# Stick-breaking and differential attention in one launch: masks of the two score components in another order, and another order of work around the first pair, the last pair and the last head

## The chip, the cores and the metric

One core of a Trainium2 chip runs the whole program, a decoder trunk of two layers on 512 tokens of width 1024, in float32. The metric is device time in microseconds, from one launch. TensorE (PE in the profile) does every product, VectorE (DVE), ScalarE (ACT) and GpSimd (POOL) prepare its operands and take its results, SyncE (SP) loads the weights.

## The reference

```python
def stick_breaking_layer(x, norm_g, w_in, w_out):
    q, k, v, gate = split(rms_norm(x, norm_g) @ w_in, 4)      # 16 heads of 64
    z = q @ k.T / 8                                           # strictly causal
    a = exp(log_sigmoid(z) + suffix_sum(log_sigmoid(-z)))
    return (silu(gate) * (a @ v)) @ w_out

def diff_layer(x, k, v, norm_g, w_in, q_norm_g, lam_params, subln_g, w_out, ...):
    q, gate = split(rms_norm(x, norm_g) @ w_in, 2)            # 8 heads, two components of 64
    q = apply_rope(rms_norm(q, q_norm_g), cos, sin)
    a = softmax(q1 @ k1.T / 8) - lam * softmax(q2 @ k2.T / 8) # causal
    o = rms_norm(a @ v, subln_g) * (1 - lam_init)
    return (silu(gate) * o) @ w_out

x = x + stick_breaking_layer(x, ...)
k, v = shared_kv(x, ...)
x = x + diff_layer(x, k, v, ...)
```

## The kernel before

Every product of float32 numbers is made of three: each operand is split into a rounded part (`..._hi`) and the rest (`..._lo`), and TensorE adds hi·hi, hi·lo and lo·hi (`three`, L637 to L639). So each slab of weights, 128 rows by 512 columns, is loaded by SyncE into `w_raw`, rounded into `w_hi` by POOL (`split`, L514) or by ACT (`slab_hi`, L1126, for the slabs in the list `ACT_HI`), and POOL subtracts it for `w_lo` (L516, or L504 behind ACT). The slabs are numbered in the order of their use; a ring of six buffers serves the first layer and a ring of four the second. All order is written by hand: each engine has its own list of work, and semaphores tie the lists together.

**The first layer** runs over eight pairs of heads. In `pair(p)` TensorE makes the scores into six banks, then the projection of this pair's gate and of the next pair's q and k. Between them stand the suffix sums of each of the two heads (`suffix_sums`, L777 and L780), which wait until DVE has written the three `lo` pieces of that head (L1711, semaphore `s_sl`), and then the products with the values (`attend_a`, L794). Before the second of these TensorE waits for `s_qk`, the split of the next pair's k (`k_lo_a`, L1640). POOL splits the values of a pair (`values_a`, L528 and L532) and six slabs for the pair after. From the second pair on, those six slabs start only after the third `lo` piece of the pair; for the first pair they start right behind the values. The last pair is written apart (`last_pair`): it has the first slabs of the output matrix between its steps.

**The second layer** runs over eight heads. Head 0 and 1 and the last two are written apart, 2 to 5 run in a loop. `head(h)` on TensorE: `scores_b(h)` puts six masks (L735, L737) into six banks and adds the scores of both components onto them (L970). Component c has the banks 2b+c for b = 0, 1, 2. Then come the projection of a gate, the values of the head before (`attend_b`), and half a projection of the q two heads on, then the turning of that projection's squares into bank 1 and of the squares of the last output into bank 3 (`turned_squares`), the turning of the probabilities into the banks of the first component (`turn_probs`), and the other half. `o_roots` spreads the roots of an output's mean squares into bank 7.

DVE in `head(h)`: for each b a maximum over the two banks (L1944) and a small product that gives ACT the bias of its exponentials (L1949, `s_nb`); `o_scale` (L1924), which scales the output two heads back and is waited for by `attend_b`; the gate; the combination of the two components' probabilities (L1960 to L1965); `o_times_gate` (L1931); the `lo` parts of the probabilities (L1996); and `turned_means`, which sums the squares in bank 1 (L1907) and bank 3 (L1909), adds the small terms (L1910, L1912: `s_rq`), and after ACT's root (`head_root`, L1131 and L1133) refines it (`newton`, L1576 to L1578: `s_rb`). `gate_log` (L1650) and `gate_silu` (L1656) are the two steps of a gate on DVE, `gate_exp` (L1242) the one of ACT between them. The gate of head 6 is the 15th; its buffers are `g32_7` and `ge_7`.

In the last head TensorE has no projection left. It makes tile after tile of the product with the output matrix (`early_tile`), two slabs, `o_roots`, two more slabs, then `attend_b`.

## Time and profile before

| | us |
|---|---|
| median of 3 runs | 626.11 (625.68 to 628.41) |
| profiled execution | 624.4 |
| its span, first to last instruction | 623.2 |
| PE busy | 604.3 (97%) |
| PE weight loads busy | 508.9 (82%) |
| DVE busy | 455.7 (73%) |
| ACT busy | 375.2 (60%) |
| POOL busy | 330.0 (53%) |
| granted TensorE clock, mean | 0.997 |

A matmul of 512 columns is listed with about 0.39 us, but they are pipelined: back to back one starts 0.23 us after another. So the time that TensorE loses at a wait is the distance of two starts less the usual step, a little more than the idle time in brackets.

### The profile page before, as it was taken

The numbers are of one execution on the slowest core, as the hardware profiler recorded it, in microseconds if no ns is written. First come the engines' busy times: TensorE is split into PE (matmuls) and PEld (weight loads), VectorE is DVE, ScalarE is ACT, GpSimd is POOL, SyncE is SP. The second block draws the span as 40 slices with busy tenths as digits, with TensorE's granted clock in tenths as the row PEclk, the third lists the DMA queues.
The fourth block names the chain that finished last, engine by engine and source line by source line (L and its number), as shares of the span: only waits on it lengthen the run. The fifth ranks groups of instructions, "written<-read, shape, count | busy, mean of one in ns | idle before, by whom it ended". The sixth has DMA issues, their size and how long they took to land.

```text
span 623.2 us, 9903 instructions
## 1 busy us (share of the span) xinstructions
PE 604.3 (97%) x3204; PEld 508.9 (82%) x3204; DVE 455.7 (73%) x734; ACT 375.2 (60%) x814; POOL 330.0 (53%) x313
## 2 busy tenths in 40 slices
PE   6999999999999999999999999999999999997998
PEld 6888887888888888878888888888878878886886
DVE  2389498988989898884337799435889888888441
ACT  5662695786968668684446644325667776685420
POOL 4639366757556475625353555557454465434261
PEclk9999999999999999999999999999999999998999
DMA  7424312213122121212212332230421222121142
GB/s 257 127 85 121 101 34 68 69 37 98 34 67 67 34 84 44 74 35 68 68 64 72 96 106 86 84 109 24 125 83 45 75 84 78 57 69 34 35 150 87
DMA packets 61439, 48.83 MB, mean 78 GB/s; under 512 B 7521, under 2 KB 48609, under 8 KB 61409
## 3 DMA queue, kind: packets, MB, share of 16 engines
q1 hardware_dynamic: 60368, 48.44, 25.4%
q8 instruction: 17, 0.28, 0.2%
q10 hardware_dynamic: 1040, 0.00, 0.1%
q14 instruction: 14, 0.11, 0.1%
HBM read 44.24 MB, written 2.10 MB: 74 GB/s over the span
## 4 chain that ended last, share of the span: by engine, by line
PE 81%; DVE 13%; issue 2%; ACT 2%; DMA 1%; POOL 0%; DVEq 0%; SPq 0%; ACTq 0%
PE bank L637 21%; PE bank L639 21%; PE bank L638 21%; PE bank L780 4%; PE bank L794 3%; PE bank L756 3%; DVE small L1944 2%; PE bank L970 1%; DVE lo L1733 1%; DVE lo L1711 1%; PE bank L777 1%; DMA xs<-in_x 1%; PE bank L990 1%; DVE sp L1697 1%; PE bank L675 1%
## 5 line engine op out<-in xcount | busy, mean ns | idle before, releaser
L504 POOL TENSOR_TENSOR w_lo<-w_raw,w_hi 128x512 fp32r<-128x512 f32 x80 | 108.5, 1368 | 154.0 <-ACT w_hi L1126 115.2
L637 PE MATMUL bank<-h_hi,w_hi 128*128 128x512 f32 x320 | 129.3, 404 | 0.7 <-ACT q L1379 0.7
L637 PE MATMUL bank<-w_hi,h_hi 128*128 128x512 f32 x320 | 127.5, 398 | 1.6 <-POOL w_lo L504 1.5
L639 PE MATMUL bank<-h_hi,w_lo 128*128 128x512 f32 x320 | 125.5, 392 | 0.0
L639 PE MATMUL bank<-w_hi,h_lo 128*128 128x512 f32 x320 | 125.1, 391 | 0.0
L638 PE MATMUL bank<-h_lo,w_hi 128*128 128x512 f32 x320 | 125.1, 391 | 0.0
L638 PE MATMUL bank<-w_lo,h_hi 128*128 128x512 f32 x320 | 124.8, 390 | 0.0
L516 POOL TENSOR_TENSOR w_lo<-w_raw,w_hi 128x512 fp32r<-128x512 f32 x80 | 112.3, 1404 | 6.4
L514 POOL CAST w_hi<-w_raw 128x512 fp32r<-128x512 f32 x80 | 59.0, 738 | 75.8 <-DVE lo L1711 35.7
L1126 ACT ACTIVATE w_hi<-w_raw 128x512 fp32r<-128x512 f32 x80 | 48.9, 630 | 55.7 <-PE bank L639 55.5
L637 PEld LDWEIGHTS bank<-h_hi,w_hi 128*128 128x128 f32 x320 | 60.1, 188 | 14.4 <-ACT q L1379 1.1
L637 PEld LDWEIGHTS bank<-w_hi,h_hi 128*128 128x128 f32 x320 | 60.1, 188 | 14.4 <-issue 2.1
L639 PEld LDWEIGHTS bank<-h_hi,w_lo 128*128 128x128 f32 x320 | 60.0, 188 | 13.6
L639 PEld LDWEIGHTS bank<-w_hi,h_lo 128*128 128x128 f32 x320 | 60.1, 188 | 13.1
L638 PEld LDWEIGHTS bank<-w_lo,h_hi 128*128 128x128 f32 x320 | 60.2, 188 | 11.8
L638 PEld LDWEIGHTS bank<-h_lo,w_hi 128*128 128x128 f32 x320 | 60.2, 188 | 11.6
L1733 DVE TENSOR_TENSOR lo<-ex,hi 128x512 fp32r<-128x512 f32 (+1 forms) x48 | 48.6, 1065 | 3.6 <-ACT hi L1280 3.6
L1506 ACT ACTIVATE pr<-bank,small 128x512 f32<-128x512 f32 (+3 forms) x64 | 38.7, 617 | 15.8 <-DVE small L1949 15.8
L1711 DVE TENSOR_TENSOR lo<-sp,hi 128x512 fp32r<-128x512 f32 (+1 forms) x48 | 41.1, 882 | 0.0
L1697 DVE SCALAR_TENSOR_TENSOR sp<-bank,ex 128x512 f32<-128x512 f32 (+1 forms) x48 | 27.3, 597 | 5.9 <-ACT ex L1263 5.6
L1831 DVE TENSOR_TENSOR xs<-bank,xs 128x512 f32<-128x512 f32 x16 | 10.9, 692 | 28.1 <-PE bank L639 28.1
L1944 DVE TENSOR_REDUCE small<-bank 128x2 f32<-128x1024 f32 (+3 forms) x32 | 25.5, 818 | 7.2 <-PE bank L970 7.2
(217 smaller groups left out, 1191.4 us busy)
## 6 DMA issues: line engine op xcount, KB each, us to landing
w_raw<-in_a_w_in SPq DMA_DIRECT2D x64, 256.0 KB, 2.8
w_raw<-in_w_kv SPq DMA_DIRECT2D x32, 256.0 KB, 3.0
w_raw<-in_b_w_in SPq DMA_DIRECT2D x32, 256.0 KB, 2.7
w_raw<-in_a_w_out SPq DMA_DIRECT2D x16, 256.0 KB, 2.6
w_raw<-in_b_w_out SPq DMA_DIRECT2D x16, 256.0 KB, 2.8
xs<-in_x SPq DMA_DIRECT2D x4, 512.0 KB, 6.1
qrot<-qs SPq DMA_DIRECT2D x32, 64.0 KB, 2.0
out_x<-xs SPq DMA_DIRECT2D x8, 256.0 KB, 2.7
```

Of the source, the lines that this page charges most:

```text
L504: nc.gpsimd.tensor_tensor(w_lo[s][:, :], w_raw[s][:, :], w_hi[s][:, :].bitcast(F32), ALU.subtract).then_inc(s_w, 1)
L514: nc.gpsimd.tensor_copy(w_hi[s][:, :], w_raw[s][:, :]).then_inc(s_whi, 1)
L516: nc.gpsimd.tensor_tensor(w_lo[s][:, :], w_raw[s][:, :], w_hi[s][:, :].bitcast(F32), ALU.subtract).then_inc(s_w, 1)
L637: pe.matmul(o, ahi, bhi, start=start, stop=False, skip_group_check=True)
L638: pe.matmul(o, ahi, blo, start=False, stop=False, skip_group_check=True)
L639: return pe.matmul(o, alo, bhi, start=False, stop=stop, skip_group_check=True)
L1126: A(w_hi[s][:, :], w_raw[s][:, :], ACT.Copy).then_inc(s_whia, 1)
L1506: A(pr[c][:, cols(at, w)], bank[BANK_B[c, b]][:, cols(at - BANKS[b][0], w)], ACT.Exp, bias=tiny[:, 8 + 2 * i + c:9 + 2 * i + c], scale=mea ...
L1697: STT(out=sp[m // 3][:, seg], in0=bank[m][:, 0:BANKS[m % 3][1]], scalar=0.0, op0=ALU.max, in1=ex[m // 3][:, seg], op1=ALU.add).then_inc(s_ ...
L1711: TTN(lo[h][:, seg], sp[h][:, seg], hi[h][:, seg].bitcast(F32), ALU.subtract).then_inc(s_sl, 1)
L1733: TTN(lo[h][:, seg], ex[h][:, seg], hi[h][:, seg].bitcast(F32), ALU.subtract).then_inc(s_al, 1)
L1944: ins = V.tensor_reduce(tiny[:, 2 * i:2 * i + 2], banks[:, 2 * b:2 * b + 2, cols(at - BANKS[b][0], w)], AX.X, ALU.max)
```

## The change

Three things are changed.

1. In `scores_b` the masks are laid in the order first component b = 0, 1, 2, then the second component's b = 2, 0, 1. The one wait for `s_rq` is gone. Bank 1 waits for a new semaphore, `s_mq` (the squares of q are summed), bank 3 for another, `s_mo` (those of the output are). `turned_means` raises them at the two sums, which now follow each other without a wait between; DVE waits for both behind them.
2. For the last head: ACT makes the root before the two slabs instead of after. DVE takes `gate_log` of the 15th gate ahead of the root's refinement, `gate_silu` of it to behind the last bias, and `o_scale` of head 5 to before the third maximum. POOL makes its two slabs before `value_lo`, and drops a wait for `s_rb`.
3. POOL, first pair: the last four of six slabs wait for `s_qk` at 4, the split of the second pair's k. POOL, last pair: the slabs from `G_OUT + 4` on wait for `s_sl` at 44, the second `lo` piece of that pair.

```diff
@@ gpsimd
-        for g in range(G_BODY + 6, G_BODY + 12):
+        split(G_BODY + 6)
+        split(G_BODY + 7)
+        pool.wait_ge(s_qk, 4)
+        for g in range(G_BODY + 8, G_BODY + 12):
             split(g)
...
         values_a(KT - 1)
+        pool.wait_ge(s_sl, (KT - 1) * 6 + 2)
         for g in range(G_OUT + 4, N_A):
             split(g)
...
-        pool.wait_ge(s_rb, KT)
-        value_lo(KT - 2)
         split(H_OUT + 2)
         split(H_OUT + 3)
+        value_lo(KT - 2)
         value(KT - 1)
@@ tensor, scores_b
-            if not first:
-                pe.wait_ge(s_rq, h + (R_HEAD - 1))
-            for c in (1, 0):
-                for b in range(3):
-                    if c == 0 and not first:
+            for c, b in ((0, 0), (0, 1), (0, 2), (1, 2), (1, 0), (1, 1)):
+                if not first:
+                    if c == 0:
                         pe.wait_ge(s_al, h * 3 + (46 + b))
-                    mask(bank[BANK_B[c, b]][:, :], (3 * P, 2 * P, P)[b], len(BANK_STRIPS[b]), P, mask_b)
+                    elif b == 0:
+                        pe.wait_ge(s_mq, h)
+                    elif b == 1 and not second:
+                        pe.wait_ge(s_mo, h - 1)
+                mask(bank[BANK_B[c, b]][:, :], (3 * P, 2 * P, P)[b], len(BANK_STRIPS[b]), P, mask_b)
@@ scalar, last head
                 gate_copies(h, later, 2 * KT - 2)
+                head_root(h - 1, False, False)
                 slab_hi(H_OUT + 2)
                 slab_hi(H_OUT + 3)
-                head_root(h - 1, False, False)
@@ vector
-            st.link(V.tensor_reduce(means[:, 0:8], comps(bank[1][:, :]), AX.X, ALU.add))
+            V.tensor_reduce(means[:, 0:8], comps(bank[1][:, :]), AX.X, ALU.add).then_inc(s_mq, 1)
             if with_o:
-                st.link(V.tensor_reduce(means[:, 8:12], bank[3].rearrange("p (t d) -> p t d", d=P), AX.X, ALU.add))
+                V.tensor_reduce(means[:, 8:12], bank[3].rearrange("p (t d) -> p t d", d=P), AX.X,
+                                ALU.add).then_inc(s_mo, 1)
+            dve.wait_ge(s_mq, h + 1)
+            if with_o:
+                dve.wait_ge(s_mo, h)
...
             for b in range(3):
+                if b == 2 and not q_next:
+                    o_scale(h - 2)
...
-            if n_before == 2:
+            if not q_next:
+                gate_silu(2 * KT - 1, g32_7, ge_7)
+            elif n_before == 2:
                 o_scale(h - 2)
...
+            if silu_first:
+                gate_log(2 * KT - 1, g32_7, ge_7)
             root_newton(c0, c1, h + R_HEAD).then_inc(s_rb, 1)
...
         head(KT - 2, 2, q_after=False, silu_first=True)
-        gate_log(2 * KT - 1, g32_7, ge_7)
-        gate_silu(2 * KT - 1, g32_7, ge_7)
```

On PE, the masks of the last head's scores (those of heads 2 to 6 alike; the line numbers of the changed file are 5 higher here), before:

```order
L735 MATMUL bank<-mask_b,ident_r 128x128 [waits norm_sum_ready,v_split,qk_split]
L737 MATMUL bank<-mask_b,ident_r 128x256
L735 MATMUL bank<-mask_b,ident_r 128x128
L735 MATMUL bank<-mask_b,ident_r 128x128 [waits weights_split]
L737 MATMUL bank<-mask_b,ident_r 128x256 [waits weights_split]
L735 MATMUL bank<-mask_b,ident_r 128x128 [waits weights_split]
```

and after:

```order
L740 MATMUL bank<-mask_b,ident_r 128x128 [waits weights_split,v_split,qk_split]
L742 MATMUL bank<-mask_b,ident_r 128x256 [waits weights_split]
L740 MATMUL bank<-mask_b,ident_r 128x128 [waits weights_split]
L740 MATMUL bank<-mask_b,ident_r 128x128
L740 MATMUL bank<-mask_b,ident_r 128x128 [waits q_squares_added]
L742 MATMUL bank<-mask_b,ident_r 128x256 [waits output_squares_added]
```

The wait that stood before all six masks, `norm_sum_ready`, is gone, and the two that replace it stand before the last two.

On DVE, between the sums of head 6 (L1910, L1912) and the first combination of the last head, before:

```order
L1576 TENSOR_TENSOR small<-small 128x12 [waits norm_root_ready]
L1577 SCALAR_TENSOR_TENSOR small<-small 128x12 [waits dve_steps]
L1578 SCALAR_TENSOR_TENSOR small<-small 128x12 [waits dve_steps]
L2006 SCALAR_TENSOR_TENSOR small<-small 128x4
L1650 SCALAR_TENSOR_TENSOR ge<-g_7,ge 128x512 [waits gate_log1p,dve_steps]
L1656 TENSOR_TENSOR silu<-g_7,ge 128x512 [waits gate_sigmoid]
L1944 TENSOR_REDUCE small<-bank 128x2 [waits scores_ready]
...
L1949 SCALAR_TENSOR_TENSOR small<-small 128x2x2 [waits dve_steps]
L1944 TENSOR_REDUCE small<-bank 128x2 [waits scores_ready]
L1949 SCALAR_TENSOR_TENSOR small<-small 128x2 [waits dve_steps]
L1924 TENSOR_TENSOR og<-ot,bank 128x512 [waits output_roots_spread]
```

and after:

```order
L1657 SCALAR_TENSOR_TENSOR ge<-g_7,ge 128x512 [waits gate_log1p]
L1583 TENSOR_TENSOR small<-small 128x12 [waits norm_root_ready]
L1584 SCALAR_TENSOR_TENSOR small<-small 128x12 [waits dve_steps]
L1585 SCALAR_TENSOR_TENSOR small<-small 128x12 [waits dve_steps]
L2023 SCALAR_TENSOR_TENSOR small<-small 128x4
L1957 TENSOR_REDUCE small<-bank 128x2 [waits scores_ready,dve_steps]
...
L1962 SCALAR_TENSOR_TENSOR small<-small 128x2x2 [waits dve_steps]
L1935 TENSOR_TENSOR og<-ot,bank 128x512 [waits output_roots_spread]
L1957 TENSOR_REDUCE small<-bank 128x2 [waits scores_ready]
L1962 SCALAR_TENSOR_TENSOR small<-small 128x2 [waits dve_steps]
L1663 TENSOR_TENSOR silu<-g_7,ge 128x512 [waits gate_sigmoid]
```

Both steps of the 15th gate have left the place between the root and the first maximum, and `og` stands one maximum and one bias earlier.

On POOL, the third and fourth of the six slabs in the first pair, before:

```order
L514 CAST w_hi<-w_raw 128x512 [waits slab_loaded5,slab_used]
L516 TENSOR_TENSOR w_lo<-w_raw,w_hi 128x512 [waits slab_hi_split]
L514 CAST w_hi<-w_raw 128x512 [waits slab_loaded0,slab_used]
L516 TENSOR_TENSOR w_lo<-w_raw,w_hi 128x512 [waits slab_hi_split]
L514 CAST w_hi<-w_raw 128x512 [waits slab_loaded1,slab_used]
```

and after:

```order
L516 CAST w_hi<-w_raw 128x512 [waits slab_loaded5,slab_used]
L518 TENSOR_TENSOR w_lo<-w_raw,w_hi 128x512 [waits slab_hi_split]
L516 CAST w_hi<-w_raw 128x512 [waits slab_used,qk_split,slab_loaded0]
L518 TENSOR_TENSOR w_lo<-w_raw,w_hi 128x512 [waits slab_hi_split]
L516 CAST w_hi<-w_raw 128x512 [waits slab_loaded1,slab_used]
```

The third slab, and with it everything that POOL has after it, waits for `qk_split`.

## Rows read from the trace of the kernel before

**Rows 1.** The page, busy time by engine and costliest groups (busy, mean ns).

```profile
PE 604.3 (97%) x3204; PEld 508.9 (82%) x3204; DVE 455.7 (73%) x734; ACT 375.2 (60%) x814; POOL 330.0 (53%) x313
...
L516 POOL TENSOR_TENSOR w_lo<-w_raw,w_hi 128x512 fp32r<-128x512 f32 x80 | 112.3, 1404 | 6.4
L514 POOL CAST w_hi<-w_raw 128x512 fp32r<-128x512 f32 x80 | 59.0, 738 | 75.8 <-DVE lo L1711 35.7
```

**Rows 2.** Waits of PE: waiting line, releaser, us in total, times, longest.

```profile
PE bank L735 <- DVE small L1912: 3.7, 6, 0.7
PE bank L637 <- DVE og L1924: 2.0, 1, 2.0
PE bank L794 <- DVE k_lo L1640: 1.5, 1, 1.5
PE bank L637 <- POOL w_lo L504: 1.5, 2, 0.8
...
PE bank L780 <- DVE lo L1711: 0.6, 1, 0.6
```

**Rows 3.** Timeline of PE, heads 3 and 4: start, duration, line, idle before.

```profile
481.83 0.39 PE L639 MATMUL bank<-h_hi,w_lo 128*128 128x512 f32 x1
482.75 0.33 PE L735 MATMUL bank<-mask_b,ident_r 128*128 128x128 f32 x1 [0.54 <-DVE small L1912]
...
483.58 0.50 PE L970 MATMUL bank<-k_hi,q_hi 64*128 64x512 f32 x2
...
500.90 0.39 PE L639 MATMUL bank<-h_hi,w_lo 128*128 128x512 f32 x1
```

**Rows 4.** Timeline of DVE, head 3.

```profile
484.95 1.23 DVE L1944 TENSOR_REDUCE small<-bank 128x2 f32<-128x1024 f32 x1 [0.57 <-PE bank L970]
...
490.96 1.06 DVE L1961 SCALAR_TENSOR_TENSOR small<-small 128x2 f32<-128x2 f32 x1
...
500.88 0.69 DVE L1909 TENSOR_REDUCE small<-bank 128x4 f32<-128x512 f32 x1
```

**Rows 5.** Timeline of POOL, head 3.

```profile
484.49 1.29 POOL L580 TENSOR_TENSOR vb_lo<-v,vb_hi 128x512 fp32r<-128x512 f32 x1 [2.24 <-DVE small L1578]
...
490.37 1.63 POOL L540 TENSOR_TENSOR k_lo<-k,k_hi 128x512 fp32r<-128x512 f32 x1 [0.19 <-POOL k_hi L538]
```

**Rows 6.** Timeline of PE, last head.

```profile
569.69 0.79 PE L637 MATMUL bank<-at_hi,vb_hi 128*128 128x512 f32 x1 [1.95 <-DVE og L1924]
...
573.10 0.44 PE L637 MATMUL bank<-w_hi,h_hi 128*128 128x512 f32 x1
...
575.89 0.95 PE L899 MATMUL bank<-small,osq 128*128 128x1 f32 x8
```

**Rows 7.** Windows: length, PE, weight loads, DVE, ACT, POOL, granted clock, DMA.

```profile
569.70:573.10 3.40, 3.40 (x13) 3.11 (x13) 2.81 (x8) 2.09 (x10) 0.00 (x0) 0.53 0.00 0
```

**Rows 8.** Timeline of DVE, last head.

```profile
565.43 1.21 DVE L1944 TENSOR_REDUCE small<-bank 128x2 f32<-128x1024 f32 x1
...
568.96 0.68 DVE L1924 TENSOR_TENSOR og<-ot,bank 128x512 f32<-128x512 f32 x1
```

**Rows 9.** Timeline of ACT, last head.

```profile
559.80 1.15 ACT L1126 ACTIVATE w_hi<-w_raw 128x512 fp32r<-128x512 f32 x2
560.84 0.21 ACT L1131 ACTIVATE small<-small 128x12 f32<-128x12 f32 x1
```

**Rows 10.** Timeline of PE, second pair of the first layer.

```profile
111.32 0.40 PE L780 MATMUL bank<-hi,neg_tri 128*128 128x512 f32 x1
```

**Rows 11.** Timeline of DVE: first and second pair; last, a later stretch without POOL.

```profile
95.05 3.61 DVE L1733 TENSOR_TENSOR lo<-ex,hi 128x512 fp32r<-128x512 f32 x3
98.58 0.68 DVE L1640 TENSOR_TENSOR k_lo<-bank,k_hi 128x512 fp32r<-128x512 f32 x1
...
109.13 0.42 DVE L1711 TENSOR_TENSOR lo<-sp,hi 128x256 fp32r<-128x256 f32 x1
...
279.01 1.63 DVE L1733 TENSOR_TENSOR lo<-ex,hi 128x512 fp32r<-128x512 f32 x3 [1.04 <-ACT hi L1280]
```

More of the change, by code:

```diff
@@ L331, in build @@
     s_or = sem("output_roots_spread")
+    s_mq = sem("q_squares_added")
+    s_mo = sem("output_squares_added")
     s_rb = sem("norm_roots_ready")
@@ L949, in _, with scores_b @@
                     turn_keys(turn_after[grp * KT + k])
-        def scores_b(h, first):
+        def scores_b(h, first, second=False):
             pe.wait_ge(s_qk, h + (2 * KT + 1))
             pe.wait_ge(s_v, KT + 1 if first else h * 2 + KT)
-            if not first:
-                pe.wait_ge(s_rq, h + (R_HEAD - 1))
-            for c in (1, 0):
-                for b in range(3):
-                    if c == 0 and not first:
-                        pe.wait_ge(s_al, h * 3 + (46 + b))
-                    mask(bank[BANK_B[c, b]][:, :], (3 * P, 2 * P, P)[b], len(BANK_STRIPS[b]), P, mask_b)
+            for c, b in ((0, 0), (0, 1), (0, 2), (1, 2), (1, 0), (1, 1)):
+                if not first:
+                    if c == 0:
+                        pe.wait_ge(s_al, h * 3 + (46 + b))
+                    elif b == 0:
[3 more added lines that the diff above has]
+                mask(bank[BANK_B[c, b]][:, :], (3 * P, 2 * P, P)[b], len(BANK_STRIPS[b]), P, mask_b)
             for b in range(3):
@@ L1019, in head @@
             if n_before:
-                scores_b(h, False)
+                scores_b(h, False, n_before == 1)
             def roots():
@@ L2017, in _ @@
         with dve.Fori(2, KT - 2) as i:
-            st.enter(i, 2, 12)
+            st.enter(i, 2, 10)
             head(i, 2)
```

4 lines of the change are left out of this document (2 added, 2 removed).

## The prediction, made before the changed kernel was timed

> **What bounds the kernel now.** I read the page first: TensorE is busy for 604.3 of 623.2 us [rows 1], so no other engine bounds the whole, and only time in which TensorE stands still can be won. Then its waits [rows 2]. Besides the first load of x, five releasers are in reach of the change: the sums of squares (3.7 us in 6 waits, one for each of heads 2 to 7), the scaled output `og` in the last head (2.0), the k split of the first pair (1.5), POOL's slabs in the last head (1.5), a `lo` piece in the last pair (0.6). Then the timelines around each, since a wait is worth what the next thing that comes late leaves of it.
>
> By the distance of starts a wait costs a little more than its listed idle time: in head 3 the last projection matmul starts at 481.83, the next could start 0.23 later, at 482.06, and the first mask starts at 482.75: 0.69 lost [rows 3].
>
> **Masks, heads 2 to 7.** In steady heads TensorE's own work from the first score matmul to the end of the projections runs from 483.58 to 500.90 + 0.23 = 501.13, 17.55 us [rows 3]. The six masks take 483.58 − 482.75 = 0.83. If nothing made it wait, a head would be 18.38; it is 19.15 now. Of the new order, the masks of three banks wait for probabilities split before the sums, so they are free at once; so is the fourth. The last waits for the second sum, which ends at 500.88 + 0.69 = 501.57 [rows 4]. Seen from that head's projection end, 501.13, five masks last to about 501.8, so in the first such head the wait goes entirely, 0.8 us.
>
> Then something else is late. DVE does not simply move up with the scores. POOL starts its chain when the root is refined (484.49), and that hangs on the end of TensorE's projection through ACT, not on the scores. DVE's small product L1961 starts at 490.96 and takes 1.06, ending at 492.02, just after POOL's `k_lo` ends at 490.37 + 1.63 = 492.00 [rows 4, 5]: it stood behind POOL. So DVE's path to the second sum is fixed to the projection end P: L1961 ends at P + 9.96, the second sum 9.55 later; the removed wait between the two sums gives 0.12 back. The sum ends at P + 19.4. The last mask starts then, the scores 0.2 later at P + 19.6. With g the time from a projection's end to the scores, the period is 17.55 + g and the scores of the next head stand at P + 17.55 + 2g, so 2g = 2.05, g about 1.03, period 18.58 instead of 19.15. That is 0.57 a head in the middle. Head by head: 0.8, 0.25 (DVE has not moved yet), 0.57 three times, and about 0.8 for the last, where DVE has slack. Sum: **3.5 us**. Bounds: 6 × 0.77 = 4.6 if TensorE bounds every head; 1.8 if only the two small terms behind the sums are saved (0.3 a head).
>
> **Last head.** Before: first maximum at 565.43, `og` from 568.96 to 569.64, values product from 569.69, 3.41 us long, to 573.10; then a tile to 575.89 and the sums of head 6's output [rows 6, 8]. After, with the projection end 2.7 earlier (3.5 less the last head's own 0.8), at 555.8: ACT copies the gate until 557.06 and makes the root at once. The two slabs cost 1.04 there before, 560.84 − 559.80 [rows 9]; they now stand behind it. DVE refines until 558.2 and finds the scores done. Gone from between are both gate steps. The first maximum starts at 558.3, 7.1 us earlier. It ends at 559.5. POOL's slab and `value_lo` chain now begins at about 558.1 and ends at about 561.9, since nothing holds it, and the bias product meets the second slab: I charge 1.1 us, as L1961 above. Second maximum and bias: 562.0. `og` one maximum earlier: 562.7. TensorE has its scores, two tile steps, the spread roots and two more steps done at 562.1 (the two slab waits, 1.5 us [rows 2], go, because the slabs no longer stand behind `value_lo` and DVE's root), so 0.7 us of waiting is left of 2.0. It starts at 562.8 instead of 569.69.
>
> The values product then: it took 3.41 us at a granted clock of 0.53, the level of 1.2 GHz, after three waits within 6 us [rows 6, 7]. With one short wait ahead I take the level of 2.4 GHz and 1.85 us. So it ends at 564.65 and the next tile at 567.45. Now DVE is late: third maximum, bias, 15th `gate_silu` (moved here, 0.6), and the combination, beside POOL's split of the last values, which may start at 564.7 and stalls two of its products for about 1.9 in all; `ot` is ready at 569.2. TensorE waits 1.75 where it did not wait. It makes the sums at 569.2 instead of 575.89: **6.7 us** earlier, of which 3.5 came from the masks and 3.2 are the last head's own. From there everything is tied to TensorE as before; the later slab of the ring stays 0.25 late as it is. Bounds: 9.1 in all if POOL stalls nothing; 4.2 if the masks give 2.5 and half the clock's 1.56 and an additional 0.7 of waiting stay.
>
> **POOL, last pair.** POOL's two slabs stood in DVE's way to the third `lo` piece; the wait is 0.6 listed [rows 2], 0.75 by starts. Held until the second piece, they meet only short operations. TensorE needs them 3 us later, after the suffix sums, with about 1 us to spare. **−0.7**, bounds −0.75 and 0.
>
> **POOL, first pair.** Here one wait goes and another comes. The k split starts at 98.58 because two groups of three `lo` pieces took 3.61 (and the one before as long) beside POOL, where three take 1.63 alone [rows 11]. With only two slabs made, the k split ends at 97.2, before TensorE comes at 97.7: −1.64 by starts (1.5 listed [rows 2]). But four slabs and the values are now made from 97.3 on. At the page's means, 1.40 + 0.74 a slab [rows 1], and 2.2 for the values, POOL is busy until about 108. That is where DVE has its stretch up to the third `lo` piece of the second pair, which ended at 109.13 + 0.42 = 109.55, with 1.77 to spare before TensorE's 111.32 [rows 10, 11]. TensorE comes at 109.68 now. DVE could be done at about 107.1; six or seven of its operations meet one of POOL's, and a meeting costs (3.61 − 1.63)/3 = 0.66, 4.3 in all: 111.4. So TensorE waits about 1.75, and all that was won is gone. DVE then runs late by 1.9 until its next k split, 16 us on: a further wait of about 0.9. Net **+1.0**. Bounds: −1.6 (DVE slips through) and +1.9.
>
> For that row the Trainium skill has a sharper price. "SBUF — State Buffer", in its section on the ports, says that a VectorE instruction with two SBUF inputs and a GpSimd one that reads SBUF exclude each other for a whole instruction, by the order of issue. Were every meeting a full slab operation, the mean of 1.40 and 0.74, the 4.3 would be 7.0 by that rule, and the first pair would come out at +3.7 instead of +1.0. The trace shows 0.66, since most meetings begin halfway, so I stay with the row.
>
> **Sum.** +1.0 − 0.7 − 6.7 = −6.4. The profiled execution took 624.4 (span 623.2): 618.0. The median of the runs is 1.7 above it, so 626.1 − 6.4 = **619.7 us**.
>
> **The rivals.**
>
> *More: POOL stalls little.* In the last head DVE's small products slip between POOL's operations, and the first pair keeps half of its 1.64. For it: half of the bias products in heads 2 and 3 are short. Against: L1961 is stalled in every head. 9.1 + 0.7 + 0.2 = 10.0: 616.1.
>
> *Less: the last head waits again.* TensorE waits for `ot` 1.75 or more after a wait for `og`, and the clock is granted at half again, as in [rows 7]. That keeps 1.56 and a second wait of 0.7: 622.0.
>
> *The masks change nothing but their place.* The second sum ends only 0.3 before the semaphore that is dropped; were the first five masks not laid meanwhile (they wait for the probabilities' split), six heads would give 1.8 instead of 3.5, and the lag would cost the last head another 1.5. 623.0. Against: those splits end 1.4 before.
>
> *Slower: DVE never catches up after the first pair.* POOL's held slabs push DVE's third `lo` piece behind TensorE's need, and if each pair has as much work for DVE as time, the lag of 1.75 returns in each of pairs 1 to 6: 6 × 1.75 − 1.64 = +8.9 against the −7.4 of the rest, 627.6. It decides from the fifth repetition. Against it: DVE idles some 2 us in each later pair, and TensorE waits for it in none of them.
>
> **How the numbers follow.** Forecast 0.50 (618 to 621.5); more 0.17; less 0.17; masks only moved 0.08; slower 0.05; something else 0.03. 615.5 reaches to the first rival, 623.0 takes in the second and third; about 0.15 is left out. What a measurement of this kernel can tell from no change is about 0.5%, 3.1 us, so 623.0. Faster by more: 0.50 + 0.17 + 0.14 + 0.03 = 0.84. Slower by more than 629.2: 0.04. Same: 0.12.
>
> **What the changed profile would show.** Right: in heads 3 to 6 the last mask, not the first, has a wait, of 0.2 to 0.4, on the second sum, and the period of the scores is near 18.6; the first maximum of the last head begins about 7 us earlier, and its values product runs at 0.23 us a matmul; a wait for `ot` of 1 to 2 us stands before the sums of head 6's output; L794 no longer waits in the first pair, but L780 waits in the second. Wrong: if heads are 18.4 long, POOL does not fix DVE's path; if they are 19.1, it is the masks' rival; if L780 doesn't wait, DVE and POOL get along better than I charge, and 1 to 2.6 us more are won; if L780 waits in several pairs, the slower rival is at work.

## The result, and the profile after

| | before | changed |
|---|---|---|
| median of 4 runs each, same chip | 627.0 us (625.68 to 628.41) | 617.25 us (617.12 to 619.89) |
| ratio, 95% interval | | 0.9869 (0.9844 to 0.9894) |
| profiled execution | 624.4 | 617.12 |
| its span | 623.2 | 615.9 |

The changed kernel is 1.3% faster, and the interval of the ratio does not reach 1. 619.7 was forecast, 617.25 came: inside the range of 615.5 to 623, but 0.75 below the band of the forecast itself (618 to 621.5). Of the profiled execution 618.0 was forecast and 617.12 came. The page of the changed kernel, with the lines that answer to [rows 1]:

```profile
PE 602.7 (98%) x3204; PEld 507.9 (82%) x3204; DVE 453.1 (74%) x734; ACT 375.5 (61%) x814; POOL 328.0 (53%) x313
...
L518 POOL TENSOR_TENSOR w_lo<-w_raw,w_hi 128x512 fp32r<-128x512 f32 x80 | 111.1, 1389 | 6.4
L516 POOL CAST w_hi<-w_raw 128x512 fp32r<-128x512 f32 x80 | 58.6, 732 | 80.4 <-DVE lo L1718 31.5
```

The same work is done in the same busy time; what went is idle time of TensorE. Its waits besides the first load of x (line, releaser: us in all, times, longest), to be read against [rows 2]:

```profile
PE bank L904 <- DVE ot L1942: 1.1, 1, 1.1
PE bank L924 <- DVE pr L1980: 1.0, 1, 1.0
PE bank L785 <- DVE lo L1718: 0.9, 1, 0.9
PE bank L642 <- ACT q L1386: 0.7, 1, 0.7
PE bank L742 <- DVE small L1916: 0.4, 2, 0.3
PE bank L642 <- DVE og L1935: 0.3, 1, 0.3
PE bank L782 <- DVE lo L1734: 0.2, 1, 0.2
```

The waits for the sums of squares (3.7), `og` (2.0), the k split (1.5), POOL's slabs (1.5) and the `lo` piece of the last pair (0.6) are gone or down to 0.4 at most. New are 1.1 for `ot`, and 0.9 and 0.2 for `lo` pieces (L1718, L1734) of the second pair. The 1.0 for `pr` was 0.8 before.

Heads 3 and 4 on TensorE, against [rows 3]: start, duration, line, idle before in brackets.

```profile
480.90 0.22 PE L740 MATMUL bank<-mask_b,ident_r 128*128 128x128 f32 x1
480.96 0.33 PE L742 MATMUL bank<-mask_b,ident_r 128*128 128x256 f32 x1
481.13 0.45 PE L740 MATMUL bank<-mask_b,ident_r 128*128 128x128 f32 x3
481.85 0.38 PE L742 MATMUL bank<-mask_b,ident_r 128*128 128x256 f32 x1 [0.27 <-DVE small L1916]
482.17 0.50 PE L977 MATMUL bank<-k_hi,q_hi 64*128 64x512 f32 x2
...
500.77 0.49 PE L977 MATMUL bank<-k_hi,q_hi 64*128 64x512 f32 x2
```

Five masks are laid without a wait, the last waits 0.27 for the second sum. The scores are 18.60 apart here. In heads 3 to 6 the last mask starts 0.23 to 0.43 later than its usual step; only two of these waits are long enough to be listed. The last head on DVE, against [rows 8]:

```profile
558.07 1.23 DVE L1957 TENSOR_REDUCE small<-bank 128x2 f32<-128x1024 f32 x1
559.33 1.16 DVE L1962 SCALAR_TENSOR_TENSOR small<-small 128x2 f32<-128x2 f32 x1
...
561.80 0.68 DVE L1935 TENSOR_TENSOR og<-ot,bank 128x512 f32<-128x512 f32 x1
...
564.25 1.64 DVE L1980 SCALAR_TENSOR_TENSOR pr<-pr,small 128x512 f32<-128x512 f32 x2
565.82 0.15 DVE L1975 RECIPROCAL small<-small 128x2 f32<-128x2 f32 x1
566.00 1.05 DVE L1976 SCALAR_TENSOR_TENSOR small<-small 128x2 f32<-128x2 f32 x1
```

and on TensorE, against [rows 6]:

```profile
562.53 0.50 PE L642 MATMUL bank<-at_hi,vb_hi 128*128 128x512 f32 x1 [0.28 <-DVE og L1935]
...
564.49 0.45 PE L642 MATMUL bank<-w_hi,h_hi 128*128 128x512 f32 x1
...
568.56 1.05 PE L904 MATMUL bank<-small,osq 128*128 128x1 f32 x8 [1.12 <-DVE ot L1942]
```

The first maximum comes 7.36 earlier (565.43 − 558.07), the values product takes 1.96 instead of 3.41, the sums of head 6's output come 7.33 earlier.

**How the runs are compared below.** The first scores of the first pair stand anywhere from 73.4 to 76.1 in these traces, whatever the kernel. In the late ones the first projections run at steps of 0.43, up to 17.7 at the latest, where the early ones have 0.23. A single time of one execution therefore tells two kernels apart only to 2.7 us. Distances between two places of one trace don't have that trouble: where an edit doesn't reach and the granted clock stays up, they repeat to 0.1. So each kernel is read by eight distances on TensorE (first score matmuls by line and shape; P is 0.23 behind the last projection matmul before the last head's masks; the sums are the sums of squares of head 6's output, the next sums those of head 7's):

| us | pair 0 to 2 | 2 to 7 | pair 7 to head 0 | head 0 to 1 | head 1 to 7 | P to values | P to sums | to next sums |
|---|---|---|---|---|---|---|---|---|
| before | 53.76 | 133.63 | 164.37 | 19.34 | 115.33 | 11.12 | 17.32 | 12.91 |
| changed | 54.11 | 133.59 | 163.56 | 19.16 | 112.50 | 6.88 | 12.91 | 12.98 |
| masks_alone | 53.71 | 133.64 | 164.41 | 19.16 | 112.47 | 11.12 | 16.59 | 12.97 |
| last_head_alone | 55.24 | 133.60 | 164.37 | 19.33 | 115.36 | 7.01 | 12.94 | 14.63 |
| first_pair_undone | 53.74 | 133.63 | 163.57 | 19.16 | 112.51 | 6.90 | 12.92 | 12.96 |
| last_pair_undone | 54.11 | 133.63 | 164.43 | 19.16 | 112.51 | 6.89 | 12.92 | 12.97 |
| hold_last_values | 54.09 | 133.59 | 163.56 | 19.16 | 112.49 | 6.89 | 11.75 | 12.97 |
| two_slabs_later | 54.01 | 135.11 | 163.56 | 19.16 | 112.52 | 6.89 | 12.91 | 14.59 |
| small_k_lo | 54.08 | 133.59 | 163.56 | 19.16 | 109.69 | 6.89 | 12.92 | 13.00 |
| masks_wait_root | 54.08 | 133.60 | 163.55 | 19.16 | 113.89 | 6.90 | 12.93 | 12.98 |
| four_slabs_first | 52.30 | 133.59 | 163.56 | 19.17 | 112.54 | 6.90 | 11.75 | 12.98 |
| three_slabs_first | 52.93 | 133.60 | 163.55 | 19.17 | 112.51 | 6.88 | 11.72 | 12.99 |
| root_late | 54.08 | 133.64 | 163.56 | 19.16 | 112.50 | 9.31 | 15.33 | 14.57 |
| gates_old_place | 54.09 | 133.59 | 163.56 | 19.16 | 112.54 | 9.19 | 15.49 | 12.92 |

Behind that, all of them need 31.5 to the last matmul. P itself moves 0.58 less than the last scores do (scores at P + 1.57 before, P + 0.99 changed), and that part of the masks' gain is not on the path, as the experiments show.

### The profile page after: what moved, and what is told of

It is laid out like the page before. It is cut to its first block, busy times and chain, and to the rows that moved or that the text cites. A ratio compares the mean times of both kernels' runs of the same rounds, so it can differ in the third digit from the quotient of the medians.

```text
span 615.9 us, 9902 instructions
## 1 busy us (share of the span) xinstructions
PE 602.7 (98%) x3204; PEld 507.9 (82%) x3204; DVE 453.1 (74%) x734; ACT 375.5 (61%) x814; POOL 328.0 (53%) x313
## 4 chain that ended last, share of the span: by engine, by line
PE 83%; DVE 11%; issue 3%; ACT 1%; DMA 1%; POOL 0%; DVEq 0%; SPq 0%; ACTq 0%
PE bank L642 22%; PE bank L644 21%; PE bank L643 21%; PE bank L785 4%; PE bank L799 3%; PE bank L761 2%; PE bank L977 2%; DVE small L1957 2%; PE bank L782 1%; DVE pr L1980 1%; DMA xs<-in_x 1%; DVE at_lo L2011 1%; PE bank L997 1%; PE bank L742 1%; DVE small L1962 1%
## 5 line engine op out<-in xcount | busy, mean ns | idle before, releaser
L642 PE MATMUL bank<-h_hi,w_hi 128*128 128x512 f32 x320 | 129.2, 404 | 0.7 <-ACT q L1386 0.7
L516 POOL CAST w_hi<-w_raw 128x512 fp32r<-128x512 f32 x80 | 58.6, 732 | 80.4 <-DVE lo L1718 31.5
L1740 DVE TENSOR_TENSOR lo<-ex,hi 128x512 fp32r<-128x512 f32 (+1 forms) x48 | 44.7, 983 | 3.7 <-ACT hi L1287 3.7
L1718 DVE TENSOR_TENSOR lo<-sp,hi 128x512 fp32r<-128x512 f32 (+1 forms) x48 | 41.0, 879 | 0.0
```

The source lines that it names most:

```text
L516: nc.gpsimd.tensor_copy(w_hi[s][:, :], w_raw[s][:, :]).then_inc(s_whi, 1)
L642: pe.matmul(o, ahi, bhi, start=start, stop=False, skip_group_check=True)
L1718: TTN(lo[h][:, seg], sp[h][:, seg], hi[h][:, seg].bitcast(F32), ALU.subtract).then_inc(s_sl, 1)
L1740: TTN(lo[h][:, seg], ex[h][:, seg], hi[h][:, seg].bitcast(F32), ALU.subtract).then_inc(s_al, 1)
```

## The experiments

### Each part alone, or undone

**masks_alone**: the kernel before with the new `scores_b` and the two semaphores of `turned_means`, nothing else.

```diff
-            for c in (1, 0):
-                for b in range(3):
+            for c, b in ((0, 0), (0, 1), (0, 2), (1, 2), (1, 0), (1, 1)):
...
+                    elif b == 0:
+                        pe.wait_ge(s_mq, h)
+                    elif b == 1 and not second:
+                        pe.wait_ge(s_mo, h - 1)
```

> Kernel before with the change to the masks alone (new order, one wait for each sum); first pair, last pair and last head as before. My sum: heads 2 to 7 give 3.5 us (period of the heads 18.6 to 18.7), the last head's values product still runs at half the granted clock, so 626.5 - 3.5 = about 623. Rival 'only their place': the last mask's wait eats it, the period stays 19.1, at most 1.8 us won. Rival 'the parts need each other': the gain of the heads is lost in the old last head, because the first maximum there waits for the root that ACT makes behind two slabs; then the first scores come 3.5 earlier but the sums of head 6's output less than 2.

Measured: 622.72 us, median of 10 (620.94 to 626.33), ratio 0.9953 (0.9926 to 0.9979). The heads take 2.86 us less from head 1 to head 7, as in the changed kernel to 0.03, and 0.18 less before that. So the masks' gain needs no other part, and "only their place" is out. But from P the values product stands at 11.12, as before: the last head's own 0.58 is not won, since DVE's first maximum (P + 6.86 in both kernels) hangs on ACT's root behind two slabs and on the two gate steps behind that, not on the scores. What I expected of the clock was wrong, so the 623 was met by two errors that offset each other: the masks gave 2.4 up to P instead of 3.5, and the full clock gave 0.73 that was not expected. TensorE's waits in the last head here:

```profile
562.35 0.47 PE L639 MATMUL bank<-w_hi,h_hi 128*128 128x512 f32 x1 [1.33 <-POOL w_lo L506]
564.03 0.47 PE L639 MATMUL bank<-w_hi,h_hi 128*128 128x512 f32 x1 [0.75 <-POOL w_lo L506]
566.93 0.50 PE L639 MATMUL bank<-at_hi,vb_hi 128*128 128x512 f32 x1 [1.96 <-DVE og L1932]
```

and the window of its values product (length, PE, weight loads, DVE, ACT, POOL, granted clock, DMA):

```profile
566.93:568.90 1.97, 1.97 (x12) 1.84 (x13) 1.67 (x4) 1.97 (x10) 0.00 (x0) 1.00 0.00 0
```

In the kernel before the same three waits were 0.77, 0.75 and 1.95. Here the first is longer, the others are equal, and the clock stayed at its upper level. The fall of [rows 7] does not follow from those waits alone.

**last_head_alone**: the kernel before with the last head's new order on DVE, ACT and POOL (POOL's `value_lo` behind the slabs, ACT's root before them, DVE's `og` one maximum earlier and the 15th gate's steps apart).

```diff
-        pool.wait_ge(s_rb, KT)
-        value_lo(KT - 2)
         split(H_OUT + 2)
         split(H_OUT + 3)
+        value_lo(KT - 2)
...
+                head_root(h - 1, False, False)
                 slab_hi(H_OUT + 2)
                 slab_hi(H_OUT + 3)
-                head_root(h - 1, False, False)
...
+                if b == 2 and not q_next:
+                    o_scale(h - 2)
```

> Kernel before with the new order of the last head alone (VectorE, ScalarE, GpSimd); masks, first and last pair as before. My theory: the first maximum comes about 3.7 us earlier (from 565.4 to 561.7), the values product starts near 566.2 at full clock, the sums of head 6's output stand near 572.2 instead of 575.89: -3.7 us. Rival: the granted clock falls to half here too, since only the masks' gain or the missing waits of the heads kept it up: then -2.1 us.

Measured: 622.23 us, median of 10 (619.55 to 624.64), ratio 0.9928 (0.9906 to 0.9951). From P to the sums 12.94, as in the changed kernel, so this part doesn't need the masks either, and the distance from scores to sums (15.75 to 11.37) is shorter by 4.4, more than the 3.7 expected. Of the 4.4, masks_alone puts 0.73 down to the lower clock of the kernel before (17.32 − 16.59). Here the clock did fall, in two other places: after the k split's wait in the first pair, and after the wait for `ot`:

```profile
100.12 0.59 PE L793 MATMUL bank<-hi,va 128*128 128x512 f32 x1 [1.51 <-DVE k_lo L1639]
...
573.80 1.05 PE L898 MATMUL bank<-small,osq 128*128 128x1 f32 x8 [1.09 <-DVE ot L1930]
574.72 2.27 PE L989 MATMUL bank<-ident,pr 128*128 128x128 f32 x10
```

```profile
100.10:103.86 3.76, 3.74 (x14) 3.18 (x16) 1.24 (x2) 0.59 (x1) 2.07 (x4) 0.55 0.51 144
...
574.70:578.00 3.30, 3.30 (x15) 3.08 (x15) 2.40 (x5) 2.10 (x4) 0.00 (x0) 0.52 0.00 0
```

Those cost 1.5 (55.24 against 53.74) and 1.65 us (14.63 against 12.98).

**first_pair_undone** and **last_pair_undone**: the changed kernel without one of POOL's two new waits.

```diff
-        split(G_BODY + 6)
-        split(G_BODY + 7)
-        pool.wait_ge(s_qk, 4)
-        for g in range(G_BODY + 8, G_BODY + 12):
+        for g in range(G_BODY + 6, G_BODY + 12):
```

> Changed kernel without the hold of GpSimd in the first pair. The prediction charged the hold with +1.0 us, the trace of the changed kernel showed a net +0.3 by the place of the first mask in the second pair. So this kernel should be 0.3 us faster than the changed one (k split waits 1.5 again, suffix sums of the second pair don't wait). Rival: the place of the mask hides a debt that is paid later (1 us or more faster), or none (then equal or slower by up to 1).

```diff
-        pool.wait_ge(s_sl, (KT - 1) * 6 + 2)
```

> Changed kernel without GpSimd's wait in the last pair. Predicted worth of the wait 0.7 us (bounds 0 and 0.75), so 0.7 us slower than the changed kernel, with the wait of 0.6 us for the third lo piece back. Rival: the scores of the first head came 0.87 us earlier in the changed kernel net of the first pair, so 0.9 slower, part of it another wait in that stretch.

Measured: 619.14 us (618.97 to 621.69) and 620.25 us (618.08 to 620.43), medians of 4. By the traces, the first pair's hold costs 54.11 − 53.74 = 0.37 and no debt is paid later (all other columns agree), the last pair's wait is worth 164.43 − 163.56 = 0.87, a little more than the 0.6 listed. As a whole first_pair_undone is not faster: its profiled execution has its first scores at 75.92, the changed kernel's at 73.72, and that accounts for its 618.97 against 617.12. The other executions have no trace. Against the kernel before, its ratio of 0.9897 (0.9859 to 0.9936) does not stand apart from the changed kernel's 0.9869 (0.9844 to 0.9894), so the 0.37 rests on the distances alone.

**masks_wait_root**: the changed kernel, the masks in the new order, but the second component waits for the small terms behind both sums.

```diff
                     elif b == 0:
-                        pe.wait_ge(s_mq, h)
-                    elif b == 1 and not second:
-                        pe.wait_ge(s_mo, h - 1)
+                        pe.wait_ge(s_rq, h + (R_HEAD - 1))
```

> Changed kernel with the new order of the masks, but the second component's first bank waits, as before the change, for the operations behind both sums instead of each bank for its own sum. It splits the gain of the masks (2.83 us from the scores of head 1 to those of head 7). Theory: the order carries most: three masks are laid meanwhile, three wait until 0.3 behind the second sum and then need 0.4 more, so about 0.5 a head is lost again of 0.57 to 0.8 in steady state by recursion, half of it by the chain: 113.7 to 114.5 instead of 112.50. Rival: the waits carry all of it, then 115.3 as before; or none, then 112.5.

Measured: 618.07 us, one run; heads 1 to 7 in 113.89, within what the theory said. The order alone is worth 115.33 − 113.89 = 1.44, a wait for each sum the other 1.39. Four masks are laid, and the fifth waits where before the first did:

```profile
482.13 0.33 PE L740 MATMUL bank<-mask_b,ident_r 128*128 128x128 f32 x1 [0.51 <-DVE small L1921]
```

### What limits the heads now

**small_k_lo**: the changed kernel, in which POOL makes only 64 of the 512 columns of `k_lo` in the heads of the second layer.

```diff
-            split_v(k32[:, bass.ds(h, 1), :]..., k_hi[:, :], k_lo[:, :])
+            waited()
+            st.link(nc.gpsimd.tensor_copy(k_hi[:, :], k32[:, bass.ds(h, 1), :]...))
+            waited()
+            nc.gpsimd.tensor_tensor(k_lo[:, 0:DH], k32[:, bass.ds(h, 1), 0:DH]...,
+                                    k_hi[:, 0:DH].bitcast(F32), ALU.subtract).then_inc(s_v, 1)
```

> Changed kernel in which GpSimd makes only 64 of 512 columns of k_lo in the heads of the second layer (the rest is left out). It tests the step that GpSimd's chain holds VectorE's path in the heads: in the changed kernel VectorE's small product L1976 took 1.06 because k_lo (1.63 us) was under way, and the heads' scores stood 18.7 apart. Theory: the product takes 0.2, VectorE's sum comes 0.85 earlier, no mask waits any more, and the period falls to TensorE's own 18.4 (scores of heads 1 to 7 in 110.4 to 111 instead of 112.50). Rival: the period comes from elsewhere (the sums' chain through TensorE and ScalarE), and stays within 0.1 of 18.7.

Measured: 616.55 us, one run; heads 1 to 7 in 109.69, five of the six periods 18.32, no mask waits any more. In the changed kernel (first fence: POOL, then DVE, of head 3) and here (second fence):

```profile
489.33 1.63 POOL L542 TENSOR_TENSOR k_lo<-k,k_hi 128x512 fp32r<-128x512 f32 x1 [0.19 <-POOL k_hi L540]
...
489.92 1.06 DVE L1976 SCALAR_TENSOR_TENSOR small<-small 128x2 f32<-128x2 f32 x1
```

```profile
490.11 0.66 POOL L584 TENSOR_TENSOR k_lo<-k,k_hi 128x64 fp32r<-128x64 f32 x1 [0.19 <-POOL k_hi L582]
...
490.70 0.22 DVE L1980 SCALAR_TENSOR_TENSOR small<-small 128x2 f32<-128x2 f32 x1
```

A product of two columns is listed with 1.06, from 489.92 to 490.98; POOL's subtraction ends at 490.96. Without it the product takes 0.22, and it is the only operation of DVE in this head whose length differs between the two kernels by more than 0.01. So the 18.6 to 18.7 of the period is not the sums' chain as such: 0.84 of DVE's path is spent behind `k_lo`, and the 2.8 us (112.50 − 109.69) are what that costs over six heads. The Trainium skill says in "SBUF — State Buffer", in the section "SBUF: two separate sides", that a VectorE instruction with two SBUF inputs and a GpSimd one that reads SBUF exclude each other: the one that starts first keeps the shared ports for its whole length. The trace agrees: POOL's subtraction starts first (489.33 against 489.92), and the product ends 0.02 behind its end.

### What holds the last head

**root_late**: the changed kernel, ACT's root behind the two slabs again.

```diff
-                head_root(h - 1, False, False)
                 slab_hi(H_OUT + 2)
                 slab_hi(H_OUT + 3)
+                head_root(h - 1, False, False)
```

**gates_old_place**: the changed kernel, DVE's two steps of the 15th gate between the root and the first maximum again.

```diff
-            if silu_first:
-                gate_log(2 * KT - 1, g32_7, ge_7)
...
+        gate_log(2 * KT - 1, g32_7, ge_7)
+        gate_silu(2 * KT - 1, g32_7, ge_7)
         head(KT - 1, 2, q_next=False, q_after=False, gate=False)
```

> Changed kernel, but ScalarE makes the last head's root behind the two slabs, as before the change. From the end of the projections the changed kernel needs 12.91 us to the sums of head 6's output (17.32 before, of it about 0.7 through the lower clock). Theory: ScalarE's order is worth its 1.04 and no more: 13.9 to 14.0. Rival: VectorE has another thing to do meanwhile (the gate step), or GpSimd's stall falls elsewhere: 13.0 to 13.4, or the early root carries most of the 3.7, then above 15.

> Changed kernel, but VectorE does the 15th gate's two steps between the root and the first maximum of the last head, as before the change. Theory: the first maximum then waits for ScalarE's gate exponential, 558.9 in the changed kernel, and starts 1.5 us later; the combination wins 0.6 back, so TensorE stands 13.6 to 14.4 from the projections' end to the sums instead of 12.91, with the values product 1.3 to 1.5 later. Rival: ScalarE, not the gate steps, set the first maximum before the change: 13.1 or less.

Measured: 621.07 and 621.96 us, one run each; from P to the sums 15.33 and 15.49 instead of 12.91. root_late was to cost 1.04 and cost 2.42, for a reason that the trace shows on DVE:

```profile
558.37 0.49 DVE L1583 TENSOR_TENSOR small<-small 128x12 f32<-128x12 f32 x1 [1.18 <-ACT small L1140]
558.89 1.22 DVE L1584 SCALAR_TENSOR_TENSOR small<-small 128x12 f32<-128x12 f32 x1
560.14 1.19 DVE L1585 SCALAR_TENSOR_TENSOR small<-small 128x12 f32<-128x12 f32 x1
...
561.44 1.23 DVE L1957 TENSOR_REDUCE small<-bank 128x2 f32<-128x1024 f32 x1
```

In the changed kernel the same three products take 0.17 or 0.18 each. One microsecond later they fall behind POOL's slabs (557.54 to 560.03) and `value_lo` (560.03 to 561.30), and each has to wait for one of POOL's instructions. The first maximum is 3.37 later. This belongs to the changed kernel, where POOL no longer waits for `s_rb`. In the kernel before, POOL was held until the refinement was done; the refinement was not stalled, and the gate steps behind it were:

```profile
561.54 0.17 DVE L1577 SCALAR_TENSOR_TENSOR small<-small 128x12 f32<-128x12 f32 x1
...
562.03 1.81 DVE L1650 SCALAR_TENSOR_TENSOR ge<-g,ge 128x512 f32<-128x512 f32 x1
...
564.53 0.98 DVE L1656 TENSOR_TENSOR silu<-g,ge 128x512 f32<-128x512 f32 x1 [0.70 <-ACT ge L1242]
```

The same two steps take 0.68 and 0.69 in the changed kernel. In gates_old_place DVE's first gate step takes 1.70 beside POOL's slabs (560.25 to 563.22), the second waits 0.70 for ACT, and the first maximum stands 5.73 behind P instead of 2.42, and the values product 2.3 later where 1.3 to 1.5 was expected. DVE gets a part of that back, since its combination no longer stands beside POOL's split: `ot` is ready at P + 14.29 against P + 12.86. That would have met the expectation of 13.6 to 14.4; the rest up to 15.49 is TensorE itself, whose clock fell from the values product on:

```profile
567.10:570.60 3.50, 3.44 (x13) 3.15 (x13) 2.88 (x10) 2.96 (x12) 0.00 (x0) 0.54 0.00 0
```

**hold_last_values**: the changed kernel, and POOL splits the last values only when DVE has combined the last probabilities.

```diff
         value_lo(KT - 2)
+        pool.wait_ge(s_cm, KT)
         value(KT - 1)
```

> Changed kernel, but GpSimd makes the last split of the values only when VectorE has combined the last probabilities. It is the test of the stall in the last head: in the changed kernel VectorE's two small or short operations took 1.64 (x2, from 564.25) and 1.05 us beside GpSimd's split from 564.83, the output times gate came at 568.5 and TensorE waited 1.12 for it. Theory 'GpSimd's split stalls them': they take 1.28 and 0.22, the wait falls to 0.3 or less, and the distance from the last head's first scores to the sums of head 6's output falls from 11.92 to about 11.1. Rival: VectorE waits for ScalarE's exponentials in any case, the distance stays within 0.2 of 11.92.

Measured: 615.6 us, one run; from P to the sums 11.75 instead of 12.91, from the scores 10.76 instead of 11.92. The wait for `ot` is gone. DVE's rows, against those of the changed kernel above:

```profile
563.93 1.28 DVE L1981 SCALAR_TENSOR_TENSOR pr<-pr,small 128x512 f32<-128x512 f32 x2
565.15 0.17 DVE L1976 RECIPROCAL small<-small 128x2 f32<-128x2 f32 x1
565.35 0.22 DVE L1977 SCALAR_TENSOR_TENSOR small<-small 128x2 f32<-128x2 f32 x1
```

1.64 and 1.05 have become 1.28 and 0.22, the sums come a further 1.16 us earlier, and it settles that POOL's split was the stall.

### The first pair, and a faster kernel

**two_slabs_later**: the changed kernel; after the k split POOL makes two slabs and the values, and the last two slabs only behind the second pair's third `lo` piece.

```diff
+        split(G_BODY + 8)
+        split(G_BODY + 9)
+        values_a(1)
+        pool.wait_ge(s_sl, 9)
+        split(G_BODY + 10)
+        split(G_BODY + 11)
...
```

> Changed kernel, but in the first pair GpSimd makes only two slabs and the values after the k split, and the last two slabs when the third lo piece of the second pair is made. Theory of the prediction (each meeting of GpSimd with VectorE costs 0.66, and the held slabs are what delays VectorE): the wait of 0.9 before the suffix sums of the second pair goes, and first scores of pair 1 to those of pair 3 take about 53.0 instead of 54.11 (53.74 without any hold). Rival: the two slabs only push the rest of GpSimd's work into the next k split, a wait stands there, and the distance is 53.7 or more.

Measured: 621.77 us, one run. The wait before the second pair's suffix sums is gone, and another stands one k split on:

```profile
PE bank L805 <- DVE k_lo L1653: 1.8, 1, 1.8
```

The rival was right (its pairs 1 and 3 are pairs 0 and 2 of the table): POOL is busy from 110.1 to 129.2 without a pause, in the stretch in which DVE has to be ready for the k split, and the last three `lo` pieces before it take 3.61 instead of 3.13. The k split starts 26.57 behind the scores of its pair, against 26.67 in the changed kernel, so DVE is hardly earlier. The debt moved, with 0.1 won, and the clock fell behind the new wait (135.11 instead of 133.6).

**four_slabs_first** and **three_slabs_first**: the changed kernel with the hold of hold_last_values, and four or three of the six slabs before the k split instead of two.

```diff
         split(G_BODY + 7)
+        split(G_BODY + 8)
+        split(G_BODY + 9)
         pool.wait_ge(s_qk, 4)
-        for g in range(G_BODY + 8, G_BODY + 12):
+        for g in range(G_BODY + 10, G_BODY + 12):
```

> Changed kernel with GpSimd's hold in the last head (as in hold_last_values) and another hold in the first pair: four of the six slabs before the k split, two after it. Theory: what costs is the amount of GpSimd's work beside VectorE's stretch on either side of the k split. VectorE stood idle for 1.82 before the k split of the changed kernel, and TensorE came 1.0 after its start; with four slabs GpSimd is busy until about 95.6 (in the time of the trace of before), the k split ends at about 97.7 and TensorE comes at 97.6; the two held slabs and the values end at about 105.5, so the third lo piece is done before TensorE needs it at 109.6. No wait of either kind: first scores of pair 0 to those of pair 2 take 52.1 to 52.5 instead of 54.11 (53.76 before), and with the last head's 1.16 the kernel takes 614.2 to 615. Rival: the debt only moves, as with two_slabs_later, and 53.7 or more stands there.

> As four_slabs_first, but three slabs before the k split and three after it. Theory: the k split is as early as in the changed kernel, and GpSimd ends its held work 2.1 earlier than there, at about 107.1: the wait before the suffix sums of the second pair falls from 0.9 to 0 to 0.3, distance 52.3 to 52.9. Rival: as for four_slabs_first.

Measured: 615.92 us, median of 5 (614.09 to 616.4), ratio 0.9819 (0.9793 to 0.9846); and 614.87 us, one run. Pair 0 to 2 takes 52.30 and 52.93, against 54.11 in the changed kernel and 53.76 before. TensorE's waits of four_slabs_first are these and the first load of x:

```profile
PE bank L927 <- DVE pr L1983: 1.0, 1, 1.0
PE bank L645 <- ACT q L1389: 0.7, 1, 0.7
PE bank L745 <- DVE small L1919: 0.5, 2, 0.3
PE bank L645 <- DVE og L1938: 0.2, 1, 0.2
```

With four slabs, three `lo` pieces take 2.12, the k split ends at 99.72 and TensorE starts at 99.78; POOL's held work ends at 107.1, and the third `lo` piece at 110.72, one microsecond before TensorE's 111.73:

```profile
97.00 2.12 DVE L1743 TENSOR_TENSOR lo<-ex,hi 128x512 fp32r<-128x512 f32 x3
99.04 0.68 DVE L1650 TENSOR_TENSOR k_lo<-bank,k_hi 128x512 fp32r<-128x512 f32 x1
...
110.30 0.42 DVE L1721 TENSOR_TENSOR lo<-sp,hi 128x256 fp32r<-128x256 f32 x1
```

615.92 is above the 614.2 to 615 expected, though the distances came as expected: its profiled execution has its first scores at 75.66. By the distances this kernel is 1.81 + 1.16 = 3.0 us better than the changed one. The two were not timed on the same chip; each has its own ratio to the kernel before, and the intervals (0.9793 to 0.9846, 0.9844 to 0.9894) hardly touch.

## Why the prediction was right, and where not

The distances add up: masks 0.18 + 2.25 up to P, last pair 0.81, first pair −0.35, last head 17.32 − 12.91 = 4.41. That is 7.30, and 7.3 is what the span lost. (P moved by 558.57 − 555.65 = 2.92: the masks and the two pairs.) The sum of the prediction was 6.4 and missed by 0.9, of which 0.65 is the first pair.

**Masks: right in the mechanism, too large.** Predicted 3.5, of which 2.7 before the last head. The table gives 2.83 for the scores of heads 2 to 7, and 2.43 with head 1's 0.18 up to P. Head by head the periods fell by 0.69, 0.05, 0.55, 0.36, 0.61, 0.57, where 0.8, 0.25, three times 0.57 and 0.8 were written. The reading that DVE's path hangs on POOL and so on the projections' end holds, as small_k_lo shows: the period is 18.32 without it, which is the 18.38 worked out for TensorE alone. The "about 0.8 for the last, where DVE has slack" moved only the scores: masks_alone has the values product at P + 11.12, as before, and in the changed kernel it is 6.88 against last_head_alone's 7.01, so 0.13 came of it. The sum of the prediction had left this 0.8 out of P (2.7 up to P, measured 2.43), so it did no harm there.

**Last head: right in the places, mis-sized in two terms.** Predicted 6.7 together with the masks, measured 7.33 by starts (with 0.46 from the two pairs, so 6.87 of the same parts). The places were met: first maximum 558.3 predicted and 558.07 measured, bias 1.1 and 1.16 behind POOL, values 562.8 and 562.53, next tile until 567.45 and about 567.3. In part that is luck, since the measured places hold the 0.46 of the two pairs and the predicted ones don't; from P, predicted at 555.8, the values product was to stand at 7.0 and stands at 6.88. `ot` came at 568.5, not 569.2: the split of the last values stalled DVE by 1.2 (1.64 − 1.28 and 1.05 − 0.22), where 1.9 was charged. The clock is the other term. The prediction takes the values product from 3.41 to 1.85, 1.56 won. masks_alone, with the same old last head at full clock, needs 16.59 from P against 17.32: only 0.73 of it lay on the path, since at full clock TensorE comes before `ot` in the old order too and waits 0.53. The order itself brought 16.59 − 12.91 = 3.68, where 2.4 were left for it (6.7 less the 2.7 up to P and the 1.56). The 3.68 are the values product 11.12 − 6.88 = 4.24 earlier, less 0.56 by which the wait for `ot` grew. The 4.24 were nearly met (4.1 predicted); the rest of the gap is that the prediction set its full wait of 1.75 for `ot` against none in the old order. The first maximum came from P + 6.86 to P + 2.42. Each of the two old orders alone keeps it at P + 5.7 to 5.8 (root_late, gates_old_place), so they don't add up.

**Last pair: right.** 0.7 predicted, 0.81 and 0.87 measured.

**First pair: right sign, a third of the size.** +1.0 predicted, +0.35 measured. The k split came as said, TensorE did wait at L785 as said, but 0.9 (1.06 by starts) rather than 1.75, and in place of the "further wait of about 0.9" only 0.2 is listed. The failed step is the charge for the meetings, 4.3 us as six or seven at 0.66. (The reading behind it was off too: the group of `lo` pieces before the one of 3.61 took 4.23, not "as long".) Five operations of DVE stand out there in the changed kernel against four_slabs_first, where POOL has two slabs fewer to make: 0.60, 1.56, 1.39, 0.97 and 0.90 against 0.43, 0.69, 0.84, 0.42 and 0.68, or 2.4 us, about 0.5 each. The Trainium skill's rule in "SBUF — State Buffer", priced at a whole instruction for each meeting, would have made the first pair +3.7. The trace does not bear that price out, although the product behind `k_lo` shows the rule itself at work. So the rival "POOL stalls little" has a share in the result: 2.4 and 1.2 us were lost where 4.3 and 1.9 were charged, though the bias product of the last head was stalled as predicted.

**The median: the last line failed.** "The median of the runs is 1.7 above it, so 626.1 − 6.4" carries the surplus over as a constant. It isn't one: the median fell by 9.75 where the profile fell by 7.3, and in the changed kernel the surplus is 0.13. Of the 2.45 us below the forecast 1.57 come from there and 0.9 from the profile's own sum. What the surplus is made of is only in part known. Two things vary between executions of one kernel: the granted clock, where each stretch at the lower level costs about 1.6 us, and the start of the program, 73.4 to 76.1. The ten executions of masks_alone look like steps of the clock: 620.9 to 621.3 at a mean of 1.000, 622.6 to 622.8 at 0.997, 624.5 to 625.6 at 0.995, one of 626.3 at 0.992. But nineteen executions of the kernel before, timed beside them, take 625.2 and 625.6 at 1.000 and anything from 625.2 to 628.4 at 0.995, so the clock alone does not order the times. Three of four executions of the changed kernel were at 1.000 and within 0.2 us, and all five of four_slabs_first were at 1.000 (614.1 to 616.4), where of nine executions of the kernel before six were at 0.995 and one at 0.994. By these means the clock fell less often once the waits were gone. How much of the 1.57 is that and how much is the start, no run shows, since only profiled executions have a trace.

## What to carry to other kernels

Where VectorE's small products and GpSimd's long ones meet, read the small ones first: a listed 1.06 or 1.22 for two or twelve columns is a wait for GpSimd, and moving an operation by 1 us can cost 2.4. A hold on GpSimd is worth choosing by amount and not only by place; two slabs, three and four before one k split gave 54.1, 52.9 and 52.3. And don't carry the surplus of a median over a profiled execution through a change that removes long waits of TensorE: such a wait can cost a part of 1.6 us beside its idle time, through the clock, and executions differ in their start as well.

## What the runs showed of the hardware

**The same wait is followed by the lower clock in one execution and not in another.** The same code with the same wait of 1.5 us at the k split kept 1.00 in three kernels (before, masks_alone, first_pair_undone) and fell to 0.55 in one (last_head_alone); after 1.8 in two_slabs_later it fell too. After the wait of 1.1 for `ot` it fell in three profiles (last_head_alone, two_slabs_later, and root_late, where 1.5 and 1.0 stood ahead) and not in five (changed, first_pair_undone, last_pair_undone, small_k_lo, masks_wait_root). After about 2.0 for `og` it fell in one of two, and after 2.5 in gates_old_place. With no wait over 0.3 in the last head (hold_last_values, four_slabs_first, three_slabs_first) it never fell there. The price is 1.5 to 1.65 us where all that follows hangs on TensorE. What decides it, these runs don't tell.

**The start of the program has no fixed length.** The first projections stood 0.23 apart from 13.30 on (changed kernel) or 0.43 apart up to 17.7 (last_pair_undone), and the first scores of the first pair stand at 73.4 to 73.9 or at 75.4 to 76.1; last_head_alone, with only a few slow steps, lies between with 74.5. The granted clock is printed as 1.00 in both, so the distances of matmuls, not that column, show the slower start. What decides it, no run here tells.

**What GpSimd does not hold up.** The maxima over 1024 columns of the banks (1.21 to 1.23) and the reciprocals (0.15 to 0.17) took the same time beside GpSimd and without it, in all these traces.
